# Two gate tiles of the differential heads moved to the end of the delta stage, and ScalarE's and VectorE's order changed there

## The chip, the cores and the metric

The kernel runs on one core of one Trainium2 chip. The metric is the device time of one execution in microseconds. Before the change it is 2049.99 us, the median of 3 runs (2049.94 to 2050.85).

## What is computed

Two transformer blocks follow one another on 512 tokens of width 1024, all in float32. The change lies in the first block. Cut to what matters there:

```python
proj = h @ w_in                        # q, k, v, z, beta, alpha of 4 delta heads; q, k, v, z of 4 differential heads
# group 1, gated delta rule, 4 heads of 128, chunk by chunk, with a state carried on:
#   solve (I + strict(k_beta k^T * decay)) [u, w] = [v_beta, k_beta e^g]
#   v_new = u - w S;  o = (q e^g) S + (q k^T * decay) v_new;  S = S e^g_last + k_dec^T v_new
o_dn = rmsnorm(o) * silu(z_dn)
# group 2, differential attention, 4 heads, query blocks of 128:
#   p = softmax(q1 k1^T) - lam * softmax(q2 k2^T)   (causal);  o = p v
o_df = rmsnorm(o) * (1 - lambda_init) * silu(z_df)
x = x + concat(o_dn, o_df) @ w_out
```

The second block (a feed-forward part, retention and sparse attention, a second feed-forward part) follows and is not touched.

## The kernel before

**Matrix products.** Every large product is made of three matmuls in a reduced float format: a high and a low part of the weights and of the activations (`mm3`, line 2015). The weights come as a stream of 304 blocks of 128 x 1024 in the order of use, into a ring of 4 buffers. SP issues their DMAs (line 796), ScalarE makes the high part (`w_split`, line 807), GpSimd the low part in four pieces (line 2529), TensorE uses them. A *unit* is one `mm3` of 128 rows of the contraction with 512 tokens; a tile of 128 output columns takes 8 units, the values of the differential heads (`dv`) 32.

**The delta stage** (some 99 to 372 us). Four chunks of 128 tokens are worked through one after another. For each chunk, TensorE makes the decay transposes and two score products (gcb, N0, A0), then inverts the triangular matrix in five levels: product Z, copied out by ScalarE (line 1064); transposes Tt, copied out by VectorE (line 1560); product dU, subtracted by VectorE (line 1567). Then come u and wT, the two half chunks with the state (wS, dS) and the output o. Each step waits for the engine before it.

**What fills the gaps.** Every engine's program calls its own `aside()` at 18 *points* per chunk, numbered on from -2 (`POINTS`, line 221). In the call of point p, TensorE (line 2105) issues in this order: the dense units due at p; the sums over squares of a head norm; at even points from 36 on also the scores S of differential step s, the transposes PT of the probabilities of step s - 2 and the product PV of step s - 3. In a level, the odd point lies between Z and dU, the even point between dU and the next Z. Which units are due where is computed in `dense_points` (line 236) from `ASIDE_DENSE` (the order of the tiles), `STRETCHES` (how many units from which point to which) and `SHARE` (weight of each of the 18 points). The order of the tiles is dqk 0, dqk 4, dz 0 to 3, dv, dqk 1, 5, 2, 6, 3, 7, z 0 to 3. `dqk` are the queries (0 to 3) and keys (4 to 7) of the differential heads, `dz` their gates, `z` the gates of the delta heads.

**ScalarE in point p** (`aside`, line 989): first `chains(p)`, line 1010: squares for norms, rsqrt of norms (Ln and Exp), at points 23, 25, 27 and 29 the silu of one `dz` tile each; at odd points from 36 on the two exponentials of step s, which wait for VectorE's maxima, and then the copy of the transposed probabilities PT of step s - 2 into `prob_t` (line 1050). After `chains`: the copy of a tile of dense results out of its PSUM bank when its last unit is due at p (line 1007), then the weight splits that have come due.

**VectorE in point p** (line 1464): scalings by finished norms; at odd points from 36 on the probabilities of step s - 1 (lines 1483 to 1490), then the maxima of step s (line 1500), then the copy of PV (line 1510).

**PSUM banks** are given out by `PLACE` (line 388). The small products of the delta stage, the sums of the head norms among them, take banks 5, 6 and 7 in turn. S uses banks 0 and 1, PT bank 2, PV bank 3, the dense tiles mostly bank 4. `begin(key)` waits until what was in the bank has been copied out.

**Norms of heads.** `norm_point(i)` gives the point of the squares of dqk tile i; the sum is one point later, the rsqrt two, the scaling three. `HO_POINT` (line 270) gives the same start for the norms of outputs: delta chunks 0 to 2 and differential heads 0 to 2 (numbered 4 to 6). The norms of delta chunk 3 and of head 7 come after the last point.

**The output projection** (372 to 423 us) multiplies eight heads' gated outputs, in the order `HEADS_OUT` (line 273): 4, 5, 6, then 0, 1, 2, 3, 7. VectorE gates a head (line 1624), ScalarE makes its high part (line 862) and VectorE its low part (line 1299). TensorE runs columns 0 to 3 over the first three heads, then columns 0 to 3 over the other five, then columns 4 to 7 over all (lines 2241 to 2245). ScalarE makes the silus of the four `z` tiles there (line 1086), one for each head, each followed by the high part of the head before.

Of the kernel before, what the change touches and what calls it, by code (L numbers as in the profile page):

```python
# [37 lines left out]
P = 128  # L38
D = 1024
KD = D // P  # L40
T = 512
# [169 lines left out]
def norms_after(j):  # L211
# [10 lines left out]
ASIDE_DENSE = [("dqk", 0), ("dqk", 4)] + [("dz", j) for j in range(4)] + [("dv", 1)] + \  # L222
    [("dqk", j + c) for j in range(1, 4) for c in (0, 4)] + [("z", j) for j in range(4)]
# [3 lines left out]
STRETCHES = [(8, -2, -2), (6, -1, -1), (82, 0, 38), (16, 39, 46), (16, 47, 54), (32, 55, 70)]  # L227
# [42 lines left out]
HO_POINT = {**{n: POINTS * (n + 1) + 2 for n in range(NQ - 1)}, **{4 + j: DF_START + 8 * j + 14 for j in range(3)}}  # L270
LATE_HEADS = [3, 7]
SILU_POINT = {23 + 2 * j: j for j in range(4)}
HEADS_OUT = [4, 5, 6, 0, 1, 2, 3, 7]
# [117 lines left out]
for _key, _ in RESULTS:  # L391
# [4 lines left out]
    elif _key in ASIDE_DENSE:  # L396
        _p = {("dv", 1): (2, 2), ("dqk", 4): (0, 1), ("dz", 1): (0, 1), ("dz", 3): (0, 1), ("dqk", 5): (2, 1)}.get(_key, (4, 1))
# [147 lines left out]
def build(nc, w_dram, x_dram, meta_dram, const_dram, small_dram, rot_dram, dec_dram, out_dram):  # L545
    with ExitStack() as ctx:
# [256 lines left out]
        def _(act):  # L803
# [206 lines left out]
            def chains(p):  # L1010

                for i in norm_at(p, 0):
                    A.sync()
                    squares([dqk[:, i, :]])
                for i in norm_at(p, 2):
                    rsqrt(("hn", 8 + i), 1.0 / 64, T)
                for i, first in HO_POINT.items():
                    if p == first and i < 4:
                        A.sync()
                        squares_chunk(i)  # L1020
                    elif p == first:
                        wait_evac(act, ("PV", i - 4, NQ - 1))
                        squares([dqk[:, i - 4, :]])
                    elif p == first + 2:
                        rsqrt(("ho", i), 1.0 / P, T)
                if p in SILU_POINT:
                    made["table"] = None
                    j = SILU_POINT[p]
                    A.own(nc.scalar.activation(dsz[:, j, :], dsz[:, j, :], ACT.Silu))
                    if j == 3:  # L1030
                        A.sync()
                        act.sem_inc(s_silu, 1)
# [3 lines left out]
                if s is not None:  # L1036
# [3 lines left out]
                    for c in range(2):  # L1040
                        A.sig(nc.scalar.activation(Sx[i][c][:, 0:w], Sx[i][c][:, 0:w], ACT.Exp, bias=mx[i][:, c:c + 1],  # L1041
                                                   accum_out=sums_[i][:, c:c + 1]), s_dfa, 2 * s + c + 1)
                e = df_at(p, 2)
# [37 lines left out]
            for i in (4, 5, 6):  # L1081
# [206 lines left out]
        def _(dve):  # L1288
# [175 lines left out]
            def aside():  # L1464
# [10 lines left out]
                if p < DF_START or (p - DF_START) % 2 == 0:  # L1475
                    return
                e = df_at(p, 1)
# [13 lines left out]
                s = df_at(p, 0)  # L1491
                if s is not None:
                    j, n, i = s // NQ, s % NQ, s % 2
                    w = (n + 1) * P
                    key = ("S", j, n)
                    if s >= 2:
                        wait_result(dve, ("PT", (s - 2) // NQ, (s - 2) % NQ))
                    wait_result(dve, key)
                    for c in range(2):
                        ins = nc.vector.tensor_tensor_reduce(Sx[i][c][:, 0:w], slot(key)[:, c * 512:c * 512 + w],  # L1500
                                                             K("causal")[:, T - w:T], 1.0, NEG, ALU.add, ALU.max, mx[i][:, c:c + 1])
                        V.own(ins) if c == 0 else V.sig(ins, *evac_at(key))
                    V.sync()
                    V.sig(nc.vector.tensor_scalar(mx[i][:], mx[i][:], -1.0, None, ALU.mult), s_df, 2 + s)
# [105 lines left out]
            def head_out(i):  # L1610
                def maker(dst, m):
# [7 lines left out]
                    if i < 4:  # L1619
                        dve.wait_ge(s_silu, 8 + 2 + i)  # L1620
# [5 lines left out]
            for part in (HEADS_OUT[0:3], HEADS_OUT[3:KD]):  # L1626
# [377 lines left out]
        def _(pe):  # L2004
# [657 lines left out]
```

## Time and profile before

| | us |
|---|---|
| median of 3 runs | 2049.99 |
| profiled execution | 2050.15 |
| its span, first to last instruction | 2048.4 |
| TensorE busy | 1994.2 (97%) |
| GpSimd busy | 936.8 (46%) |
| VectorE busy | 863.3 (42%) |
| ScalarE busy | 735.9 (36%) |

The mean granted TensorE clock is 0.995 of full speed. In the profile's rows PE is TensorE's matmuls, PEld its weight loads, DVE VectorE, ACT ScalarE, POOL GpSimd. The first line number is that of the kernel; many matmuls have line 2013, that of a helper, and are told apart by their tiles. The delta stage's tiles have names of their own buffers: `dn_y` is the copy of Z, `dn_inv_t` U, `dn_inv` Tt, `dn_qg` the exponential of gcb, `score` and `mx` the differential scores and maxima, `slot` is any PSUM bank. A row of the timeline has start, duration, engine, line and operation, and in brackets how long the engine was idle before it and what ended that. The starts of matmuls tell more than their durations, since one begins while the one before still drains.

### The profile page before, as it was taken

To read this page: it belongs to the slowest core of one execution; us is meant where nothing else is said; L and a number is where in the kernel's file an instruction comes from. 1 tells how busy PE (TensorE), PEld (TensorE's weight loads), DVE (VectorE), ACT (ScalarE), POOL (GpSimd) and SP (SyncE) were. 2 spreads that over 40 slices of the span, in tenths; PEclk is the share of its full clock that TensorE was granted. 3 is DMA by queue.
4 is the path that set the end of the run, shared out by engine and by line. 5 is a ranking of instruction groups with operands and counts; after the bars stand their busy time and mean duration, and the time that the engine had idled before them with its cause. 6 is when DMAs were issued, how large, how long until landed. Compare 5 with 4: busy or idle time off the path is not lost.

```text
span 2048.4 us, 30374 instructions
## 1 busy us (share of the span) xinstructions
PE 1994.2 (97%) x11366; PEld 1704.6 (83%) x11366; DVE 863.3 (42%) x1502; ACT 735.9 (36%) x1116; POOL 936.8 (46%) x1220
## 2 busy tenths in 40 slices
PE   7999988999999999999999999999999999999998
PEld 6688666799999999688888888888888888888887
DVE  7744665742222222996443233343343452222112
ACT  5543444432222223634444233333333332222222
POOL 5432211454444564554332545444444564545564
PEclk9999999999999999999999999999999999999999
DMA  5211100122222223222111322222222223222232
GB/s 186 83 62 42 42 32 32 50 95 85 93 88 92 97 99 114 73 83 79 58 61 52 109 72 88 83 78 83 84 77 77 91 90 102 92 92 93 103 103 83
DMA packets 49754, 168.68 MB, mean 82 GB/s; under 512 B 6400, under 2 KB 8576, under 8 KB 49664
## 3 DMA queue, kind: packets, MB, share of 16 engines
q1 hardware_dynamic: 46192, 161.37, 23.4%
q10 hardware_dynamic: 3472, 6.03, 0.9%
q8 instruction: 66, 1.08, 0.2%
q14 instruction: 24, 0.20, 0.0%
HBM read 165.29 MB, written 2.10 MB: 82 GB/s over the span
## 4 chain that ended last, share of the span: by engine, by line
PE 87%; DVE 8%; ACT 2%; issue 1%; DMA 1%; ACTq 0%; DVEq 0%
PE slot L2013 86%; DVE ix_score L1835 1%; DVE square L1770 1%; DVE score L1500 0%; DVE x_lo L1788 0%; DVE xt L1780 0%; ACT score L1041 0%; PE slot L2150 0%; DMA h<-x_t 0%; PE slot L2185 0%; PE slot L2448 0%; DVE dqk L1343 0%; DMA w_raw<-weights 0%; DVE aq L1773 0%; DVE ak L1773 0%
## 5 line engine op out<-in xcount | busy, mean ns | idle before, releaser
L2529 POOL TENSOR_TENSOR w_lo<-w_raw,w_hi 128x256 fp32r<-128x256 f32 x1216 | 936.6, 802 | 1100.9 <-ACT w_hi L814 848.4
L2013 PE MATMUL slot<-x_hi,w_hi 128*128 128x264 f32 (+1 forms) x1864 | 643.9, 345 | 3.5 <-ACT dqk L1007 3.4
L2013 PE MATMUL slot<-x_hi,w_lo 128*128 128x264 f32 (+1 forms) x1864 | 630.5, 338 | 0.0
L2013 PE MATMUL slot<-x_lo,w_hi 128*128 128x264 f32 (+1 forms) x1864 | 628.8, 337 | 0.0
L2013 PEld LDWEIGHTS slot<-x_hi,w_hi 128*128 128x128 f32 x1864 | 351.4, 189 | 50.7 <-issue 7.9
L2013 PEld LDWEIGHTS slot<-x_lo,w_hi 128*128 128x128 f32 x1864 | 350.9, 188 | 39.2
L2013 PEld LDWEIGHTS slot<-x_hi,w_lo 128*128 128x128 f32 x1864 | 351.7, 189 | 37.8 <-issue 1.4
L814 ACT ACTIVATE w_hi<-w_raw 128x1024 fp32r<-128x1024 f32 x216 | 226.4, 1054 | 321.4 <-PE slot L2013 311.6
L2013 PE MATMUL slot<-f_hi,w_hi 128*128 128x264 f32 (+2 forms) x550 | 173.5, 316 | 0.0
L2013 PE MATMUL slot<-f_hi,w_lo 128*128 128x264 f32 (+2 forms) x550 | 173.3, 315 | 0.0
L2013 PE MATMUL slot<-f_lo,w_hi 128*128 128x264 f32 (+2 forms) x550 | 172.9, 314 | 0.0
L1682 DVE TENSOR_TENSOR xt<-slot,rs 128x528 f32<-128x528 f32 (+1 forms) x44 | 30.8, 700 | 218.2 <-PE slot L2013 218.2
L2013 PEld LDWEIGHTS slot<-f_lo,w_hi 128*128 128x128 f32 x550 | 103.5, 188 | 7.1
L2013 PEld LDWEIGHTS slot<-f_hi,w_hi 128*128 128x128 f32 x550 | 103.5, 188 | 7.0
L2013 PEld LDWEIGHTS slot<-f_hi,w_lo 128*128 128x128 f32 x550 | 103.3, 188 | 6.5
L2013 PE MATMUL slot<-w_hi,x_hi 128*128 128x512 f32 (+1 forms) x288 | 103.1, 358 | 4.2 <-DVE ak L1773 4.2
L895 ACT ACTIVATE f_hi<-xt 128x528 f32 (+3 forms) x44 | 28.1, 639 | 217.0 <-DVE xt L1685 217.0
L2013 PE MATMUL slot<-w_hi,x_lo 128*128 128x512 f32 (+1 forms) x288 | 98.9, 343 | 0.0
L2013 PE MATMUL slot<-w_lo,x_hi 128*128 128x512 f32 (+1 forms) x288 | 98.8, 343 | 0.0
L1708 DVE SCALAR_TENSOR_TENSOR h<-slot,h 128x528 f32<-128x528 f32 (+2 forms) x17 | 11.4, 668 | 192.7 <-PE slot L2013 192.7
L883 ACT ACTIVATE w_hi<-w_raw 128x1024 fp32r<-128x1024 f32 x88 | 91.9, 1044 | 0.0
L2013 PE MATMUL slot<-mixed_hi,w_hi 128*128 128x512 f32 x168 | 69.8, 415 | 11.4 <-POOL w_lo L2529 9.4
(342 smaller groups left out, 2819.3 us busy)
## 6 DMA issues: line engine op xcount, KB each, us to landing
w_raw<-weights SPq DMA_DIRECT2D x304, 512.0 KB, 3.2
h<-x_t ACTq DMA_DIRECT2D x4, 512.0 KB, 6.1
dec<-decays ACTq DMA_DIRECT2D x4, 264.0 KB, 3.2
const<-consts SPq DMA_DIRECT2D x1, 576.0 KB, 6.4
at_rot<-rotations ACTq DMA_DIRECT2D x1, 528.0 KB, 5.1
ix_rot<-rotations ACTq DMA_DIRECT2D x1, 528.0 KB, 6.6
rt_rot<-rotations ACTq DMA_DIRECT2D x1, 528.0 KB, 3.7
out<-h SPq DMA_DIRECT2D x2, 256.0 KB, 2.2
```

Source lines behind the costliest of these rows:

```text
L814: nc.scalar.activation(w_hi[b % RING][:], w_raw[b % RING][:], ACT.Copy).then_inc(s_hi, 1)
L883: nc.scalar.activation(w_hi[b % RING][:], w_raw[b % RING][:], ACT.Copy).then_inc(s_hi, 1)
L895: nc.scalar.activation(f_hi[:, g * 2 + (first + j), c0:TT], xt[j][:, c0:TT], ACT.Copy).then_inc(s_xhi, 1)
L1682: nc.vector.tensor_tensor(oo, psu, nn, ALU.mult).then_inc(evac_in(up, g)[0], 1)
L1708: V.sig(nc.vector.scalar_tensor_tensor(hh, src, 0.5, hh, ALU.mult, ALU.add), *evac_at(key))
L1770: V.own(nc.vector.tensor_tensor(other[rows], other[rows], tab(1)[rows], ALU.mult))
L1835: ins = nc.vector.scalar_tensor_tensor(score[n - 1][:, 0:w], relu[s % 2][:, a, 0:w], iw[:, n, 2 * j + a:2 * j + a + 1], before, ALU.mult, ...
L2013: return nc.tensor.matmul(out, lhsT, rhs, start=start, stop=stop)
L2529: nc.gpsimd.tensor_tensor(w_lo[j][:, piece], w_raw[j][:, piece], w_hi[j][:, piece].bitcast(F32), ALU.subtract).then_inc(s_lo, 1)
```

## The change

The tiles dz 2 and dz 3 leave their place ahead of `dv` and come after dqk 7; the stretches are set anew. Their silus move from the delta stage to the output projection, whose first part takes two heads instead of three. ScalarE's `chains` is split up: in a point, the copy into `prob_t` now comes first, then the rsqrts, the dense copies and weight splits, then the squares (those of the next point) and the silus, and the exponentials last. VectorE makes the maxima of step s before the probabilities of step s - 1. The norms of the heads' outputs 4 to 6 start one point later.

```diff
-ASIDE_DENSE = [("dqk", 0), ("dqk", 4)] + [("dz", j) for j in range(4)] + [("dv", 1)] + \
-    [("dqk", j + c) for j in range(1, 4) for c in (0, 4)] + [("z", j) for j in range(4)]
+ASIDE_DENSE = [("dqk", 0), ("dqk", 4)] + [("dz", 0), ("dz", 1), ("dv", 1)] + \
+    [("dqk", j + c) for j in range(1, 4) for c in (0, 4)] + [("dz", 2), ("dz", 3)] + [("z", j) for j in range(4)]
-STRETCHES = [(8, -2, -2), (6, -1, -1), (82, 0, 38), (16, 39, 46), (16, 47, 54), (32, 55, 70)]
+STRETCHES = [(8, -2, -2), (6, -1, -1), (66, 0, 38), (16, 39, 44), (16, 45, 50), (48, 51, 70)]
-HO_POINT = {**{n: POINTS * (n + 1) + 2 for n in range(NQ - 1)}, **{4 + j: DF_START + 8 * j + 14 for j in range(3)}}
+HO_POINT = {**{n: POINTS * (n + 1) + 2 for n in range(NQ - 1)}, **{4 + j: DF_START + 8 * j + 15 for j in range(3)}}
-SILU_POINT = {23 + 2 * j: j for j in range(4)}
-HEADS_OUT = [4, 5, 6, 0, 1, 2, 3, 7]
+SILU_POINT = 23
+LATE_SILUS = [0, 1, 6, 2, 3, 7]
+HEADS_OUT = [4, 5] + LATE_SILUS
+OUT_FIRST = 2
...
-        _p = {("dv", 1): (2, 2), ("dqk", 4): (0, 1), ("dz", 1): (0, 1), ("dz", 3): (0, 1), ("dqk", 5): (2, 1)}.get(_key, (4, 1))
+        _p = {("dv", 1): (2, 2), ("dqk", 4): (0, 1), ("dz", 1): (0, 1), ("dqk", 5): (2, 1)}.get(_key, (4, 1))
...
-                chains(p)
+                prob_copy(p)
+                rsqrts(p)
                 for key in ASIDE_DENSE:
                     if dense_done(key) == p:
...
                 w_split(BLOCK[ASIDE_DENSE[0]] + aside_blocks(p + 1) + RING - 1)
+                all_squares(p)
+                exps(p)
...
+            def all_squares(p):
+
+                for i in norm_at(p, -1):
+                    A.sync()
+                    squares([dqk[:, i, :]])
+                for i, first in HO_POINT.items():
+                    if p == first - 1 and i < 4:
                         A.sync()
                         squares_chunk(i)
-                    elif p == first:
+                    elif p == first - 1:
                         wait_evac(act, ("PV", i - 4, NQ - 1))
                         squares([dqk[:, i - 4, :]])
+                if p == SILU_POINT:
                     made["table"] = None
+                    for j in range(2):
+                        A.own(nc.scalar.activation(dsz[:, j, :], dsz[:, j, :], ACT.Silu))
+                    A.sync()
+                    act.sem_inc(s_silu, 1)
...
-            for i in (4, 5, 6):
+            for i in HEADS_OUT[0:OUT_FIRST]:
                 x_high(1, i, M, mixed_hi)
             rsqrt(("ho", 7), 1.0 / P, T)
             made["table"] = None
-            for j in range(4):
-                A.own(nc.scalar.activation(sz[:, :, j, :], sz[:, :, j, :], ACT.Silu))
+            for i, hd in enumerate(LATE_SILUS):
+                z = sz[:, :, hd, :] if hd < 4 else dsz[:, hd - 4, :]
+                A.own(nc.scalar.activation(z, z, ACT.Silu))
                 A.sync()
                 act.sem_inc(s_silu, 1)
-                if j:
-                    x_high(1, j - 1, M, mixed_hi)
-            for i in (3, 7):
-                x_high(1, i, M, mixed_hi)
+                if i:
+                    x_high(1, LATE_SILUS[i - 1], M, mixed_hi)
+            x_high(1, LATE_SILUS[-1], M, mixed_hi)
...
             for j in range(4):
-                out_part(j, 0, 3)
+                out_part(j, 0, OUT_FIRST)
             for j in range(4):
-                out_part(j, 3, KD)
+                out_part(j, OUT_FIRST, KD)
```

On VectorE the block of the probabilities (`e = df_at(p, 1)`, lines 1477 to 1490) moves behind the block of the maxima (`s = df_at(p, 0)`, lines 1491 to 1504), unchanged; and `head_out` waits for the silu of every head in `LATE_SILUS`.

## Rows read from the trace of the kernel before

**Rows 1.** Windows: length, busy (count) of PE, PEld, DVE, ACT, POOL, PEclk, DMA, GB/s

```profile
109.90:161.70 51.80, 50.77 (x303) 42.24 (x302) 26.42 (x40) 17.44 (x26) 18.11 (x23) 1.00 0.19 63
161.70:213.80 52.10, 51.13 (x325) 44.28 (x324) 24.26 (x39) 18.43 (x26) 12.21 (x16) 1.00 0.14 50
213.80:291.30 77.50, 68.26 (x392) 51.63 (x391) 46.37 (x116) 37.18 (x78) 15.23 (x20) 0.98 0.10 35
291.30:372.00 80.70, 71.89 (x413) 56.08 (x411) 48.62 (x127) 34.99 (x77) 15.99 (x20) 0.94 0.09 29
...
396.00:423.00 27.00, 27.00 (x125) 22.40 (x124) 26.58 (x30) 8.21 (x10) 22.26 (x23) 1.00 0.37 124
```

**Rows 2.** TensorE's waits, 214 to 291 us: total, times, longest

```profile
PE slot L2150 <- ACT prob_t L1050: 3.7, 4, 1.6
PE slot L2013 <- ACT dqk L1007: 3.4, 1, 3.4
PE slot L2013 <- ACT square L834: 1.2, 1, 1.2
PE slot L2013 <- ACT dn_y L1064: 0.7, 1, 0.7
```

**Rows 3.** TensorE's waits from 291 to 372 us

```profile
PE slot L2150 <- ACT prob_t L1050: 4.7, 4, 2.1
PE slot L2013 <- ACT dn_qg L1059: 2.3, 1, 2.3
```

**Rows 4.** Timeline around one such wait, VectorE, ScalarE and TensorE

```profile
253.62 0.75 DVE L1489 SCALAR_TENSOR_TENSOR score<-score,sum 128x512 f32<-128x512 f32 x1
...
254.83 0.17 DVE L1504 TENSOR_SCALAR mx<-mx 128x2 f32<-128x2 f32 x1
...
255.81 0.47 ACT L1050 ACTIVATE prob_t<-slot 128x384 f32<-128x384 f32 x1
...
256.43 0.63 PE L2150 MATMUL slot<-const,score 128*128 128x128 f32 x4 [0.71 <-ACT prob_t L1050]
```

**Rows 5.** Windows with a lowered granted clock (the number after POOL's count)

```profile
280.00:285.00 5.00, 4.75 (x16) 3.40 (x16) 0.00 (x0) 2.35 (x4) 2.80 (x4) 0.67 0.00 0
296.00:302.00 6.00, 4.63 (x18) 3.19 (x19) 5.72 (x9) 4.47 (x8) 3.17 (x4) 0.73 0.01 3
...
357.00:364.00 7.00, 7.00 (x26) 5.91 (x26) 3.17 (x7) 0.33 (x1) 0.00 (x0) 0.53 0.00 0
...
377.00:381.00 4.00, 4.00 (x12) 3.03 (x11) 2.15 (x4) 3.70 (x6) 0.00 (x0) 0.57 0.02 4
```

**Rows 6.** Timeline of TensorE: a half step with one unit, and a sum over squares

```profile
132.44 0.39 PE L2013 MATMUL slot<-x_hi,w_lo 128*128 128x512 f32 x1
132.67 0.40 PE L2013 MATMUL slot<-x_lo,w_hi 128*128 128x512 f32 x1
133.19 1.13 PE L2013 MATMUL slot<-dn_y,dn_inv 128*128 128x128 f32 x8
...
317.43 1.02 PE L2013 MATMUL slot<-square,const 128*128 128x512 f32 x2
318.28 1.05 PE L2013 MATMUL slot<-dn_y,dn_inv 128*128 128x128 f32 x8
```

**Rows 7.** Timeline of TensorE, the first Z of chunk 1

```profile
170.10 1.13 PE L2013 MATMUL slot<-dn_inv_t,dn_join 128*128 128x128 f32 x8 [0.72 <-DVE dn_qg L1552]
```

**Rows 8.** Timeline of VectorE, the copy of U0 in chunk 3

```profile
304.54 0.69 DVE L1555 COPY dn_inv_t<-slot 128x512 f32<-128x512 f32 x1 [0.34 <-PE slot L2177]
```

**Rows 9.** Timeline of the output projection, VectorE and TensorE

```profile
382.66 0.68 DVE L1299 TENSOR_TENSOR mixed_lo<-xt,mixed_hi 128x512 fp32r<-128x512 f32 x1
...
383.98 0.69 DVE L1299 TENSOR_TENSOR mixed_lo<-xt,mixed_hi 128x512 fp32r<-128x512 f32 x1
...
385.87 0.39 PE L2013 MATMUL slot<-mixed_hi,w_hi 128*128 128x512 f32 x1
...
386.10 1.47 DVE L1299 TENSOR_TENSOR mixed_lo<-xt,mixed_hi 128x512 fp32r<-128x512 f32 x2
```

More of the change, by code:

```diff
@@ L1008, in aside, with rsqrts @@
                 w_split(BLOCK[ASIDE_DENSE[0]] + aside_blocks(p + 1) + RING - 1)
[L1010 to L1014, printed above, removed]
+                all_squares(p)
+                exps(p)
+            def rsqrts(p):
                 for i in norm_at(p, 2):
@@ L1017, in chains, with exps @@
                 for i, first in HO_POINT.items():
-                    if p == first and i < 4:
+                    if p == first + 2:
+                        rsqrt(("ho", i), 1.0 / P, T)
+            def all_squares(p):
[4 more added lines that the diff above has]
+                    if p == first - 1 and i < 4:
                         A.sync()
                         squares_chunk(i)
-                    elif p == first:
+                    elif p == first - 1:
                         wait_evac(act, ("PV", i - 4, NQ - 1))
                         squares([dqk[:, i - 4, :]])
-                    elif p == first + 2:
-                        rsqrt(("ho", i), 1.0 / P, T)
-                if p in SILU_POINT:
+                if p == SILU_POINT:
                     made["table"] = None
[L1028 to L1032, printed above, removed]
+                    for j in range(2):
+                        A.own(nc.scalar.activation(dsz[:, j, :], dsz[:, j, :], ACT.Silu))
+                    A.sync()
+                    act.sem_inc(s_silu, 1)
+            def exps(p):
                 if p < DF_START or (p - DF_START) % 2 == 0:
@@ L1042, in chains, with prob_copy @@
                                                    accum_out=sums_[i][:, c:c + 1]), s_dfa, 2 * s + c + 1)
+            def prob_copy(p):
+                if p < DF_START or (p - DF_START) % 2 == 0:
+                    return
                 e = df_at(p, 2)
@@ L1476, in aside @@
                     return
-                e = df_at(p, 1)
-                if e is not None:
-                    j, n, i = e // NQ, e % NQ, e % 2
-                    w = (n + 1) * P
-                    dve.wait_ge(s_dfa, 2 * e + 2)
-                    V.own(nc.vector.reciprocal(sums_[i][:], sums_[i][:]))
-                    V.sync()
-                    V.own(nc.vector.tensor_scalar(sums_[i][:, 1:2], sums_[i][:, 1:2], lamt[:, 5:6], None, ALU.mult))
-                    V.sync()
-                    V.own(nc.vector.tensor_scalar(Sx[i][1][:, 0:w], Sx[i][1][:, 0:w], sums_[i][:, 1:2], None, ALU.mult))
-                    V.sync()
-                    V.sig(nc.vector.scalar_tensor_tensor(Pm[i][:, 0:w], Sx[i][0][:, 0:w], sums_[i][:, 0:1], Sx[i][1][:, 0:w],
-                                                         ALU.mult, ALU.add), s_dfp, e + 1)
                 s = df_at(p, 0)
@@ L1504, in aside @@
                     V.sig(nc.vector.tensor_scalar(mx[i][:], mx[i][:], -1.0, None, ALU.mult), s_df, 2 + s)
+                e = df_at(p, 1)
+                if e is not None:
+                    j, n, i = e // NQ, e % NQ, e % 2
+                    w = (n + 1) * P
+                    dve.wait_ge(s_dfa, 2 * e + 2)
+                    V.own(nc.vector.reciprocal(sums_[i][:], sums_[i][:]))
+                    V.sync()
+                    V.own(nc.vector.tensor_scalar(sums_[i][:, 1:2], sums_[i][:, 1:2], lamt[:, 5:6], None, ALU.mult))
+                    V.sync()
+                    V.own(nc.vector.tensor_scalar(Sx[i][1][:, 0:w], Sx[i][1][:, 0:w], sums_[i][:, 1:2], None, ALU.mult))
+                    V.sync()
+                    V.sig(nc.vector.scalar_tensor_tensor(Pm[i][:, 0:w], Sx[i][0][:, 0:w], sums_[i][:, 0:1], Sx[i][1][:, 0:w],
+                                                         ALU.mult, ALU.add), s_dfp, e + 1)
                 e = df_at(p, 3)
@@ L1618, in maker @@
                         V.sync()
-                    if i < 4:
-                        dve.wait_ge(s_silu, 8 + 2 + i)
+                    if i in LATE_SILUS:
+                        dve.wait_ge(s_silu, 8 + 2 + LATE_SILUS.index(i))
                     z = sz[:, :, i, :] if i < 4 else dsz[:, i - 4, :]
@@ L1625, in head_out @@
                 return maker
-            for part in (HEADS_OUT[0:3], HEADS_OUT[3:KD]):
+            for part in (HEADS_OUT[0:OUT_FIRST], HEADS_OUT[OUT_FIRST:KD]):
                 split([head_out(i) for i in part], M, 0, mixed_hi, mixed_lo, part)
```

## The prediction, made before the result was known

> **What bounds the kernel now.** I read first the busy time by stage, then the list of TensorE's waits in the last two chunks of the delta stage, then the order of time around some of those waits. The windows [rows 1] cut the delta stage at the transposes that open its four chunks: 51.8, 52.1, 77.5 and 80.7 us. In chunks 0 and 1 TensorE lacks 1.0 us each of being busy throughout, in chunk 2 it lacks 9.2, in chunk 3 8.8. From 396 us on it is busy without a gap, and the change touches nothing there: what can be won is idle time and slow clock before that point.
>
> The waits of chunk 2 [rows 2] and chunk 3 [rows 3] name the causes. Eight waits of the differential transposes on the copy of the previous transposed probabilities (prob_t) cost 3.7 + 4.7 us; one wait for a tile copied out of its PSUM bank (dqk) 3.4; squares of a chunk 1.2; the copy of the delta's Z (dn_y) 0.7; the exponential that frees the bank of gcb (dn_qg) 2.3. One such wait in order of time [rows 4]: VectorE ends the probabilities at 254.37 and the maxima at 255.00, only then ScalarE takes the two exponentials and, behind them, the copy (255.81), and TensorE starts its transposes at 256.43. The copy's own input had been there since the even point before: it stands behind the exponentials only by its place in ScalarE's program.
>
> Idle time is not all. The granted clock [rows 5] was 0.67 for 5 us after the 3.4 us wait, 0.73 for 6 us around the 2.3 us wait, 0.53 for 7 us late in chunk 3 and 0.57 for 4 us in the output projection, which is 1.6, 1.6, 3.3 and 1.7 us of lost work (length times one minus the clock); these are stretches at 1.2 GHz among others at 2.4.
>
> **Prices.** A dense unit is three matmuls of 512 columns, which start 0.23 us apart (132.44 to 132.67): 0.69 us [rows 6]. A sum over squares takes TensorE 0.85 us (317.43 to 318.28) [rows 6]; I take 0.9 with its start. I counted units and sums by laying the table of points out. The dense units go from 38, 36, 38, 34 in chunks 0 to 3 to 31, 30, 45, 40: 13 units, 8.9 us, leave the first two and enter the last two. (The two tiles are 16 units; the end of the dv tile and of dqk shift with the new stretches.) The sums go from 6 to 8 in chunk 2 and from 5 to 3 in chunk 3.
>
> **Chunk 0: -4.1 us.** 7 units leave: -4.8. In a half step with one unit TensorE waits for the copies: its last dense matmul starts at 132.67 and would hand over 0.23 later, the next one starts at 133.19, so 0.3 us are lost [rows 6]. There are two more such half steps: +0.6. A unit before the first Z saves only half, since that Z waits for VectorE: +0.35. One unit more ahead of the chunk's output covers a wait of about 0.3 there.
>
> **Chunk 1: -1.4 us.** 6 units leave: -4.1. Two of them stood before the first Z, which already waited 0.72 for VectorE [rows 7], so they save nothing: +1.4. Three half steps fall to one unit: +0.9. One before the last output also: +0.4. From both sides: chunks 0 and 1 together give between 0 (VectorE and ScalarE bound them as soon as cover goes) and -8.9 (units alone); I take -5.5, nearer the units, since the gap that [rows 6] show with one unit is less than half of a unit.
>
> **Chunk 2: -2.5 us.** The probability copy now comes first in its point, a point before it is needed: -3.7. The dense copies come before the exponentials: the dqk wait, -3.4, and its slow clock, -1.6. Squares move to the end of the point before: -1.2. Z's copy no longer has a chain of table load and squares before it: -0.7. Against that 7 units +4.8 and 2 sums +1.8. New waits: a sum now stands right behind the transposes of gcb at the chunk's start and needs their bank, the situation that cost 2.3 in chunk 3. Here two dense units stand before it in both cases, but no differential probabilities delay VectorE yet, so it is nearer to half: I take 1.0, and 0.5 for the maximum that S of the next point waits for. Bounds 0 and 2.8.
>
> **Chunk 3: -6.0 us.** Waits -4.7 and -2.3 (no sum stands there any more); slow clock -1.6 and -3.3; 2 sums -1.8; 6 units +4.1. At the chunk's start VectorE is the bound: its copy of U0 at 304.54, which the first Z needs, follows an idle time of only 0.34 [rows 8], and its work there does not shrink; two head scalings now even fall between gcb and T. TensorE, with one wait and two sums fewer, arrives early and waits: +2.4, between 0 and 3. A wait of that size was followed by a slow stretch three times [rows 5]; I book 1.2, as part of it lies beside VectorE's work; bounds 0 and 3.3.
>
> In both chunks VectorE takes the maxima before the probabilities, which makes the latter later by the maxima: 0.63 us in [rows 4], where the block is the narrowest, and by my estimate from that up to 1.4 where it is four times as wide. There it is covered: probabilities were ready 2.06 us before the transposes that used them. The maxima, and so the exponentials, come earlier, and the exponentials, though now behind a dense copy and a weight split, are needed two points later. Booked at nothing, covered by the 2 or 3 dense units and the S of the even point; with no cover it would be the third rival.
>
> **Output projection: +2.0 us.** The first part now has 2 heads (8 units, 5.5 us) instead of 3, the second six. VectorE makes a head each 1.32 us (382.66 to 383.98) [rows 9], TensorE uses one in 0.69 us for a column. So the first column waits. ScalarE drops one copy before the last rsqrt, so the first late head comes sooner, but it is one head more, and the last low part stays where it was, at 387.57 [rows 9]. The first column then ends a unit after that part is ready, at 388.3, instead of 389.3 (385.87 [rows 9] plus 5 units), and the three others have a unit more each, 2.1: +1.1. The short waits may add a slow stretch to the one shown: 0 to 1.7, I take 0.9. The silus removed at points 27 and 29 hid under matmuls there, so they give nothing; at the end two more silus on ScalarE hide beside VectorE's 1.32 per head.
>
> **Queues.** The weight blocks keep their number; two of them move behind dqk 7 in the stream, with their DMA on SP, the split on ScalarE and four subtractions on GpSimd. No row of [rows 2, 3] is a wait for the low part, so I book nothing; if it were late, TensorE's first unit of a tile would show it. One tile moves from bank 0 to bank 4; it must wait for the copy of the tile before, which has a Z, dU or output matmul in between: nothing.
>
> **Sum.** -4.1 - 1.4 - 2.5 - 6.0 + 2.0 = -12.0 us. The profiled execution took 2050.15 (span 2048.4 and 1.75 around it), 0.16 above the median of 2049.99. 2050.15 - 12.0 = 2038.15, or 2038.0 against the median; I forecast **2038.0**.
>
> **Rivals.** A difference under 0.2% (4.1 us) can't be told from none here.
> 1. The first two chunks give nothing, as their chain bounds them once the cover is thin: +5.5, 2043.5. For it: chunk 1 starts with a wait for VectorE already [rows 7]. Against: the gap of [rows 6] is 0.3. Chance 0.14.
> 2. VectorE becomes the bound of chunks 2 and 3, so that half of the eight waits (4.2) come back under its name, with a slow stretch or two (3.3): 2045.5, on the border. For it: 48.6 us busy of 80.7 [rows 1], in one chain with TensorE. Chance 0.12.
> 3. Slower: the probabilities, now behind the maxima, are what each of the 16 transposes waits for. Price up to 16 x 1.1 = 17.6: 2055.5. It decides from 0.8 us a transpose on. Against: the 2.06 us of [rows 4]. Chance 0.04.
> 4. The short waits in the thinned chunks 0 and 1 bring the clock down. Each fall costs 1.6 to 3.3 us, so three would give about 2045, eight would cancel all. Against: the granted clock was 1.00 over both chunks [rows 1] although half steps with such gaps were there. The Trainium skill (TensorE: Matmul & The Clock Gate, A second HAM failure mode) says that frequent micro-idles between groups of matmuls can make the clock swing though the engine looks busy; by that rule the thinning is harmful, and no run here shows it at gaps of 0.3 us. Chance 0.06.
> 5. All waits go and none of the new ones comes (no slow stretch at chunk 3's start or in the projection, no wait for VectorE): -12.0 - 1.2 - 0.9 - 2.4 - 1.5 = -18.0, 2032.0. Chance 0.14.
> The copies could also fail to come earlier, if their input came only in their own point; the order of the program (transposes in the even point, copy in the odd one) excludes it.
>
> My forecast (2035 to 2042) has 0.5. The range 2031.5 to 2046.0 takes in rivals 1 and 5 and the better parts of 2 and 4. Faster 0.85 (the forecast, 1, 5 and the better half of 2), the same 0.10 (the rest of 2, most of 4), slower 0.05 (3, and the worst of 4).
>
> **What would show it.** Right: no wait of the transposes on prob_t but in the last point, no wait on dqk; chunk 0 near 47.7, chunk 1 near 50.7, chunk 2 near 75, chunk 3 near 74.5 us; a wait for VectorE ahead of chunk 3's first Z; waits on mixed_lo in the first column. Wrong: waits of transposes on the probabilities (VectorE), a clock below 1.00 in chunks 0 or 1, or a projection later than 2 us.

## The result, and the profile after

The changed kernel takes **2039.09 us** (median of 5 runs), the kernel before 2049.94 beside it: ratio 0.9946, 95% interval 0.9935 to 0.9957. The forecast was 2038.0 with a range of 2031.5 to 2046.0. The profiled execution took 2037.25 (span 2035.5), 12.9 less than the 2050.15 of before; the steps below are measured against these two. It is the shortest of its five executions (2037.25 to 2040.2), so the steps sum to 2.0 more than the 10.85 us by which the medians differ. Of the 12.9, 0.5 come from ahead of the delta stage, which the change doesn't touch; over all the profiles below that point, the start of chunk 0, lies between 109.19 and 110.59 us.

First a correction of my own reading. The cut at 213.80 in [rows 1] lies 1.5 us late: chunk 2's transposes of gcb start at 212.26. Chunk 3 had been cut at 372.00 instead of at its last product with the values (370.50). The forecasts of the chunks' lengths are to be read from these cuts: the changes in length of the prediction give 47.7, 49.2, 76.6 and 73.2 us. The windows of before with all cuts made alike:

```profile
161.70:212.26 50.56, 49.59 (x312) 42.74 (x310) 23.39 (x37) 17.09 (x24) 12.21 (x16) 1.00 0.15 52
212.26:291.33 79.07, 69.83 (x405) 53.17 (x404) 47.27 (x118) 38.52 (x79) 15.23 (x20) 0.98 0.10 34
291.33:370.50 79.17, 70.36 (x403) 54.89 (x402) 48.30 (x126) 34.38 (x77) 15.99 (x20) 0.94 0.08 27
370.50:396.00 25.50, 23.45 (x93) 17.64 (x94) 19.29 (x28) 15.57 (x23) 5.29 (x6) 0.93 0.07 21
```

And the windows of after, which answer to them and to [rows 1] (length, busy time of PE, PEld, DVE, ACT, POOL, then the granted clock):

```profile
109.36:156.99 47.63, 46.32 (x282) 38.14 (x281) 25.32 (x40) 15.62 (x23) 14.62 (x19) 1.00 0.20 65
156.99:206.68 49.69, 46.57 (x293) 38.99 (x292) 24.98 (x37) 18.33 (x25) 13.01 (x16) 1.00 0.12 37
206.68:283.81 77.13, 74.70 (x430) 57.18 (x429) 48.53 (x123) 39.18 (x83) 15.65 (x20) 1.00 0.11 40
283.81:357.05 73.24, 69.58 (x418) 55.69 (x416) 47.69 (x120) 32.86 (x73) 18.74 (x24) 0.98 0.11 37
357.05:382.00 24.95, 21.33 (x86) 15.10 (x87) 19.67 (x29) 16.60 (x25) 5.89 (x6) 1.00 0.08 25
```

The third window is to be read as a pair with its row of before: TensorE is busy 4.87 us longer, and idle 2.43 us instead of 9.24. The moved work and the filled gaps nearly cancel. What is left of the waits in the stage and the projection, against [rows 2, 3]:

```profile
PE slot L2029 <- DVE mixed_lo L1315: 3.3, 4, 1.5
PE slot L2029 <- DVE dn_qg L1568: 2.3, 1, 2.3
PE slot L2029 <- DVE mx L1502: 1.9, 1, 1.9
PE slot L2029 <- ACT rs L853: 1.6, 1, 1.6
PE slot L2029 <- ACT prob_t L1066: 1.2, 1, 1.2
...
PE slot L2166 <- DVE score L1519: 0.3, 1, 0.3
```

The eight waits of the transposes (8.4 us under a helper's line of their own, now 2166) are gone, and so are dqk, dn_y and the long dn_qg of ScalarE; the prob_t left is that of the last product with the values. In order of time, one round as in [rows 4], then the waits that are left:

```profile
252.16 0.59 ACT L1066 ACTIVATE prob_t<-slot 128x512 f32<-128x512 f32 x1
...
253.52 0.17 DVE L1506 TENSOR_SCALAR mx<-mx 128x2 f32<-128x2 f32 x1
254.36 0.35 DVE L1519 SCALAR_TENSOR_TENSOR score<-score,sum 128x128 f32<-128x128 f32 x1
...
255.85 0.50 ACT L1052 ACTIVATE score<-score,mx 128x256 f32<-128x256 f32 x1
...
279.61 0.60 ACT L1088 ACTIVATE qkv<-slot 128x512 f32<-128x512 f32 x1 [5.54 <-PE slot L2029]
280.10 0.48 ACT L1066 ACTIVATE prob_t<-slot 128x384 f32<-128x384 f32 x1
280.47 0.69 ACT L853 ACTIVATE rs<-slot,eps 128x512 f32<-128x512 f32 x1
281.22 1.16 PE L2029 MATMUL slot<-xt,dn_kdec 64*128 64x128 f32 x8 [1.64 <-ACT rs L853]
...
296.22 0.92 PE L2029 MATMUL slot<-dqk 64*128 64x384 f32 x4 [1.92 <-DVE mx L1502]
297.44 0.33 PE L2166 MATMUL slot<-const,score 128*128 128x128 f32 x1 [0.31 <-DVE score L1519]
...
361.90 0.47 PE L2029 MATMUL slot<-mixed_hi,w_hi 128*128 128x512 f32 x1 [1.46 <-DVE mixed_lo L1315]
```

The copy of the probabilities (252.16) now comes 1.36 us ahead of the maxima. The row at 281.22 is the one wait that I hadn't seen coming: the second half chunk's product for the state (dS) needs a bank that holds sums of squares, and the rsqrt that frees it stands in ScalarE's program behind the copy of the chunk's output (279.61), which is itself late work of that chunk.

### The profile page after: what moved, and what is told of

It reads as the page before. It is cut to its first block, busy times and chain, and to the rows that moved or that the text cites. A ratio compares the mean times of both kernels' runs of the same rounds, so it can differ in the third digit from the quotient of the medians.

```text
span 2035.5 us, 30377 instructions
## 1 busy us (share of the span) xinstructions
PE 1991.9 (98%) x11366; PEld 1702.1 (84%) x11366; DVE 863.6 (42%) x1502; ACT 735.5 (36%) x1116; POOL 939.7 (46%) x1220
## 4 chain that ended last, share of the span: by engine, by line
PE 91%; DVE 5%; ACT 2%; issue 1%; DMA 1%; ACTq 0%; DVEq 0%
PE slot L2029 90%; DVE x_lo L1804 0%; DVE square L1786 0%; DVE xt L1796 0%; DMA h<-x_t 0%; PE slot L2464 0%; PE slot L2201 0%; DVE dqk L1359 0%; PE slot L2166 0%; ACT rs L853 0%; DMA w_raw<-weights 0%; DVE qkv L1409 0%; DVE ak L1789 0%; DVE ix_score L1851 0%; DVE xt L1640 0%
```

## The experiments

The kernel's time is split at the same points in each profile: the start of each chunk's gcb transposes, the last product with the values (chunk 3's end), the first matmul of the projection, and the logarithm of FFN 1's norm ("projection" is the time between these last two). From there to the end every kernel takes 1619.3 to 1620.0; between chunk 3's end and the projection lie 4.9 us in all but order_best2 (6.3). Each row is one execution, and executions of one kernel differ: those of order_both_back run from 2043.28 to 2049.48. A difference of 2 us between two rows is therefore read together with the medians.

| kernel | chunk 0 | 1 | 2 | 3 | projection | span | median, ratio [95%] |
|---|---|---|---|---|---|---|---|
| before | 51.80 | 50.56 | 79.07 | 79.17 | 53.16 | 2048.4 | |
| after | 47.63 | 49.69 | 77.13 | 73.24 | 54.09 | 2035.5 | 2039.09, 0.9946 [0.9935, 0.9957] |
| order_alone | 51.78 | 50.55 | 72.52 | 70.87 | 52.33 | 2032.1 | 2032.52, 0.9911 [0.9894, 0.9927] |
| tiles_alone | 47.69 | 51.21 | 86.63 | 81.57 | 54.10 | 2056.2 | 2058.01, 1.0044 [1.0029, 1.0058] |
| projection_alone | 51.81 | 50.55 | 80.68 | 79.15 | 56.22 | 2052.5 | 2053.29, 1.0015 [1.0006, 1.0025] |
| copy_last | 47.61 | 49.72 | 78.44 | 72.03 | 54.10 | 2035.9 | 2038.51, 0.9944 [0.9927, 0.9961] |
| maxima_second | 47.69 | 49.72 | 77.36 | 74.04 | 54.10 | 2037.1 | 2039.26, 0.9947 [0.993, 0.9963] |
| norm_point_undone | 47.65 | 49.73 | 75.44 | 71.31 | 54.10 | 2031.9 | 2034.86, 0.9929 [0.9912, 0.9945] |
| old_tiles_copy_behind | 51.81 | 50.55 | 72.30 | 70.40 | 52.30 | 2031.6 | 2035.09, 0.9934 [0.9917, 0.9951] |
| old_tiles_exps_early | 51.79 | 50.55 | 73.60 | 70.88 | 52.33 | 2033.8 | 2036.17, 0.9934 [0.9917, 0.9951] |
| order_both_back | 51.80 | 50.53 | 76.45 | 78.13 | 52.33 | 2044.0 | 2046.66, 0.9986 [0.9976, 0.9996] |
| order_sum_table | 51.75 | 50.54 | 69.55 | 68.34 | 52.30 | 2027.6 | 2029.48, 0.9901 [0.9885, 0.9918] |
| order_best2 | 51.78 | 50.54 | 69.50 | 68.11 | 52.79 | 2028.3 | 2030.18, 0.9906 [0.989, 0.9923] |

**The two halves of the change.** First the new order alone, on the tiles, stretches and projection of before (with it VectorE's maxima ahead of the probabilities):

```diff
-                chains(p)
+                prob_copy(p)
+                rsqrts(p)
...
+                all_squares(p)
+                exps(p)
```

> The kernel before with the changed order of ScalarE and VectorE alone (tiles, stretches, silus and the projection's order as before). Theory 1, the order and the moved tiles both earn: the waits of the transposes on prob_t and the one on dqk go (8.4 and 3.4 us, with 1.6 and 3.3 of slow clock), but with 13 units less in the last two chunks TensorE comes to VectorE's and ScalarE's results early and waits about 0.5 us a level (10 levels), so the time is 2041 to 2044, later than the full change. Theory 2, the order earns all and the tiles' move only shifts work: 2033 to 2037, earlier than the full change, as the first chunks lose 5 us but the last two carry 8.9 us of units and the projection 0.9 less. Chunks 0 and 1 are 51.8 and 50.6 us in both.

Then the tiles, stretches, silus and projection of after under the old order of ScalarE and VectorE (on after, the same edit the other way round):

```diff
-                prob_copy(p)
-                rsqrts(p)
+                chains(p)
...
-                all_squares(p)
-                exps(p)
```

> The full change with the old order on ScalarE and VectorE (copy into prob_t behind the exponentials and ahead of the dense copies, squares at a point's start, probabilities before maxima). Theory 1: chunks 0 and 1 stay at 47.6 and 49.7 us; in chunks 2 and 3 the waits on prob_t shrink with the cover from 8.4 to some 3 us, the wait for a dense copy (3.4) stays or comes at several tiles; 2045 to 2049. Theory 2: no gain at all or a loss, 2049 to 2054. Either way waits of the transposes on prob_t are back in the list.

The order alone gives 16.3 us by the profiles and 18.2 by the medians (2032.52 beside 2050.7); the tiles alone (the shifted norms are in it) cost 7.8 and are slower outside the interval. On the new tiles the order is worth 20.7 (2056.2 to 2035.5). Both lie outside what was expected: the order a little under the 2033 to 2037 of its second theory, the tiles (2058.01) above even the 2049 to 2054 of theirs. TensorE's waits between 205 and 400 us, first of the order alone, then of the tiles alone:

```profile
PE slot L2031 <- ACT dn_qg L1076: 2.2, 1, 2.2
PE slot L2031 <- DVE mixed_lo L1317: 2.0, 3, 1.5
PE slot L2031 <- ACT dn_y L1081: 2.0, 1, 2.0
PE slot L2031 <- ACT prob_t L1067: 1.2, 1, 1.2
```

```profile
PE slot L2029 <- ACT dqk L1012: 6.2, 2, 3.7
PE slot L2166 <- ACT prob_t L1066: 4.8, 5, 1.6
PE slot L2029 <- ACT qkv L1012: 3.7, 1, 3.7
...
PE slot L2029 <- DVE mx L1516: 2.2, 2, 1.7
...
PE slot L2029 <- ACT dsz L1012: 1.2, 1, 1.2
```

With the old order the added units of chunks 2 and 3 buy little: prob_t waits fall from 8.4 to 4.8 us, but copies of dense tiles, of which there are more there now, are awaited four times (dqk twice, qkv and dsz, a dz tile, once each) for 11.1 us in place of 3.4. The longest, in ScalarE's order: the dense copy stands behind exponentials that themselves waited for the maxima.

```profile
233.38 0.61 ACT L1052 ACTIVATE score<-score,mx 128x384 f32<-128x384 f32 x1 [2.98 <-DVE mx L1520]
...
234.59 0.25 ACT L1066 ACTIVATE prob_t<-slot 128x128 f32<-128x128 f32 x1
234.75 0.58 ACT L1012 ACTIVATE dqk<-slot 128x512 f32<-128x512 f32 x1
...
235.38 0.79 PE L2029 MATMUL slot<-x_hi,w_hi 128*128 128x512 f32 x1 [3.69 <-ACT dqk L1012]
```

Chunk 1 of tiles_alone took 51.21 us where 49.7 was expected. Its waits are those of after, the same one of 2.3 us ahead of the first Z; but here a lowered clock followed it, where after has 1.00 from 165 to 170:

```profile
166.71 2.05 PE L2029 MATMUL slot<-dn_inv_t,dn_join 128*128 128x128 f32 x8 [2.31 <-DVE dn_qg L1568]
```

```profile
165.00:170.00 5.00, 3.29 (x12) 3.03 (x13) 2.21 (x3) 0.60 (x1) 2.80 (x3) 0.66 0.22 60
```

**The projection alone**: on before, only the later silus and the new split of the heads.

```diff
-SILU_POINT = {23 + 2 * j: j for j in range(4)}
-HEADS_OUT = [4, 5, 6, 0, 1, 2, 3, 7]
+SILU_POINT = {23: 0, 25: 1}
+LATE_SILUS = [0, 1, 6, 2, 3, 7]
+HEADS_OUT = [4, 5] + LATE_SILUS
+OUT_FIRST = 2
```

> The kernel before with the projection's change alone: first part over two heads, the silus of dz 2 and dz 3 at the end. The delta stage keeps its lengths (51.8, 50.6, 79.1, 79.2). From the first matmul of the projection to the rsqrt of the first feed-forward part it was 53.2 us before (with 1.7 of slow clock) and is 54.1 in the full change (no slow clock). By my sum the projection costs 1.1 without the clock and up to 2.0 with it: 2051 to 2053. If the clock is what decides, the interval is 54.1 again and the time 2050.5 to 2052; if the projection cost nothing, 53.2 or less and 2049 to 2051.

The stretch takes 3.06 us more than before, and 2.12 more than the same code in after; mixed_lo waits are 3.3 us in both. Of these 2.12, 1.7 are the clock: 0.73 in this window of projection_alone and 0.93 in the next five microseconds, while after has 1.00 over the whole stretch. The time, 2053.29, is just above the 2051 to 2053 expected; its ten executions run from 2049.36 to 2055.18.

```profile
386.00:391.00 5.00, 3.86 (x12) 2.64 (x11) 3.60 (x7) 1.44 (x2) 0.00 (x0) 0.73 0.00 0
```

(The 80.68 of its chunk 2 against 79.07, with the same waits, lie outside the edit.)

**Which element of the order?** Each was taken back by itself in the changed kernel: the probability copy behind the exponentials,

```diff
-                prob_copy(p)
                 rsqrts(p)
...
                 exps(p)
+                prob_copy(p)
```

> The full change with one thing undone: the copy into prob_t stands last in ScalarE's point again, behind dense copies, squares and exponentials. If the place of this copy was the cause of the eight waits, they come back, 4 to 10 us in chunks 2 and 3 together with slow clock, 2043 to 2050. If the better cover and the earlier maxima hide them anyway, it is within 2 us of the full change, 2037 to 2041.

and VectorE's probabilities ahead of the maxima (the two blocks swapped back):

```diff
+                e = df_at(p, 1)
...
                 s = df_at(p, 0)
...
-                e = df_at(p, 1)
```

> The full change with one thing undone: VectorE makes the probabilities before the maxima again. My sum booked this order at nothing. If so, 2037 to 2041, with the wait on the maxima at chunk 3's start (1.9 us) a little longer, 3 us, as they come later. If the maxima first is what hides the exponentials, waits on mx or on exponentials come at many points and it is 2042 or more. If it had cost something (probabilities late), the 0.3 us wait on score goes and it is 0.3 to 1 us faster.

Neither makes a difference that can be told from after: 2038.51 and 2039.26. In copy_last the copy's waits come back at 1.7 us (three of them), and the wait for the maxima at chunk 3's start falls by as much, from 1.9 to 0.2; in maxima_second chunk 3 starts on the maxima 3.0 us late instead of 1.9. The same was then asked on the old tiles, where there is less cover in chunks 2 and 3; first the copy behind (the edit of copy_last, on order_alone),

> order_alone with the copy into prob_t last in ScalarE's point, so without the cover of the moved tiles. In the full change this place cost nothing over the whole (1.7 us of waits on prob_t against 1.7 less on the maxima). If the copy's place matters once TensorE has 34 to 38 units instead of 40 to 45, waits of the transposes on prob_t of 4 to 8 us are back and it takes 2036 to 2041. If it was never the place of the copy but the wait for the dense copies and the maxima, it stays within 2 us of order_alone, 2031 to 2035.

then the exponentials ahead of the dense copies:

```diff
                 rsqrts(p)
+                exps(p)
...
                 all_squares(p)
-                exps(p)
```

> order_alone with the exponentials ahead of the dense copies, weight splits and squares (the copy into prob_t stays first). If the dense copies' place behind the exponentials is the dear part of the old order (waits of 3.4 us on a dense tile, with slow clock), chunk 2 gets one or two of them back, 4 to 8 us: 2037 to 2041. If the copy into prob_t was the dear part, it stays at 2031 to 2035.

The copy behind brings back 2.5 us of prob_t waits in four places, yet its profile (2031.6) is no longer than that of the order alone (2032.1). The clock hides it: around the waits on dn_y and dn_qg, which both kernels have, order_alone ran at 0.86 and 0.80 (226 to 236) and at 0.66 (290 to 295), old_tiles_copy_behind at 1.00 each time. The medians (2035.09, 2032.52) are 2.6 apart, with overlapping intervals. So this place of the copy costs about 2.5 us, which lies between the two expectations. The exponentials ahead bring back half of the dqk wait (1.7 us, before 3.4): 1.7 us by the profiles, 3.6 by the medians (its executions, 2034.99 to 2037.43, all lie above those of order_alone, 2031.26 to 2033.90). So no single element that was taken back carries the 16 us. The theory that was left: the probabilities, the maxima, the exponentials and the copy stood in one chain over two engines, and cutting it in one place does most of it. It was tested with both taken back at once, on order_alone (the edits of copy_last and maxima_second together):

> The order change alone, but with two of its elements taken back at once: VectorE takes the probabilities ahead of the maxima again, and ScalarE copies the transposed probabilities behind the exponentials again. The squares stay at the end of the point before, and the copies of dense tiles stay ahead of the exponentials. Theory 'one chain, cut at two places': VectorE's probabilities, its maxima, ScalarE's exponentials and the copy stood in one chain before the differential transposes; each of the two elements alone had cut it, so the wait comes back only when both are taken back. Then waits of the transposes on prob_t of 5 to 8.4 us in chunks 2 and 3 (8.4 before), at least four of them, and a time of 2039 to 2044 us, that is 4 to 8 us above the order change alone (2032.5). Rival 'neither matters; the squares and the dense copies ahead of the exponentials earn it all': prob_t waits stay at 2.5 us or less, as with the copy alone taken back, and the time is 2032 to 2036 us. A wait on the copied bank (dqk) is expected by neither.

```profile
PE slot L2168 <- ACT prob_t L1067: 10.0, 10, 2.2
PE slot L2031 <- ACT dn_qg L1076: 2.2, 1, 2.2
PE slot L2031 <- ACT dn_y L1081: 2.0, 1, 2.0
```

The waits are back in full, ten of them, and the time is 2046.66, 2.7 us above what the chain theory had said and far outside its rival. There are ten waits and not eight; here the copy stands behind the dense copies too, as it didn't in before, which may be why. Taken back one at a time the elements cost 2.6 us (the copy, on the old tiles) and nothing that can be told (the copy and the maxima, on the new tiles); together they are worth 14 us by the medians (2046.66 to 2032.52) and 12 by the profiles. The maxima alone on the old tiles were not run, so it is not excluded that there the maxima's place alone carries most of it. The rest of the gain, 3.2 us (2046.66 to 2049.88), is of the size that the exponentials ahead of the dense copies cost alone; the moved squares were not taken back by themselves.

**The wait that I had not seen coming**, in after: the norms of heads 4 to 6 back to their old point, so that their sums don't share point 52 with another sum.

```diff
-{4 + j: DF_START + 8 * j + 15 for j in range(3)}
+{4 + j: DF_START + 8 * j + 14 for j in range(3)}
```

> The full change with the norms of heads 4 to 6 one point earlier again, so that point 52 has one sum and not two. If the unforeseen wait of 1.6 us on an rsqrt at the end of chunk 2 comes from two sums there and the bank that one of them holds until ScalarE's rsqrt behind the output copy, it goes, chunk 2 is 75.3 to 76 us long and the time 1 to 2 us below the full change, 2036 to 2038. If it comes from the bank rotation as such, the wait moves to another product and chunk 2 stays at 77.

The wait of 1.64 us is gone and chunk 2 is 1.69 shorter. Chunk 3 is 1.93 shorter, though it waits for the maxima as long as in after. The median, 2034.86, is below the 2036 to 2038 expected, and its executions (2033.72 to 2036.2) all lie below those of after. The window behind that wait in after, and the same stretch with the wait in norm_point_undone:

```profile
296.00:301.00 5.00, 4.47 (x20) 3.73 (x21) 4.75 (x18) 2.52 (x6) 2.00 (x3) 0.68 0.01 2
```

```profile
292.00:297.00 5.00, 2.78 (x18) 1.75 (x17) 4.75 (x16) 2.52 (x6) 0.01 (x1) 1.00 0.01 2
297.00:302.00 5.00, 5.00 (x31) 4.15 (x30) 4.27 (x12) 2.40 (x6) 2.84 (x4) 1.00 0.17 54
...
294.20 0.92 PE L2029 MATMUL slot<-dqk 64*128 64x384 f32 x4 [1.91 <-DVE mx L1502]
```

**A version that beats both.** The waits that order_alone has left point to it: a sum directly behind the chunk's transposes (dn_qg, 2.2) and a load of ScalarE's function table (1.28 us) in the chain ahead of Z's copy (dn_y, 2.0).

```diff
-    return p + 1 if (p + 1) % POINTS == POINTS - 1 else p
+    return p + 2 if (p + 1) % POINTS == POINTS - 1 else p
...
+                if made["table"] != LN_EXP:
+                    nc.scalar.preload_act_table_set(LN_EXP)
+                    made["table"] = LN_EXP
                 act.wait_ge(s_dn, dnv("dt", n))
```

> The order change alone with two small edits: the sum of differential head 3's norm stands a point later (point 55 in place of 54, so behind the first Z of chunk 3 and not directly behind its gcb transposes, with its copies and rsqrt a point later), and the table of exp and ln is loaded ahead of the chunk's own exponentials in the first chunk point of a round, not ahead of the norm's logarithm. Theory: the wait of 2.2 us at the start of chunk 3 (290.82, released by the exponential of gcb) goes with the slow stretch behind it, and the Z copy's wait (dn_y 2.0 in chunk 2) falls to about 0.7: chunk 3 is 68 to 69.5 us instead of 70.87, chunk 2 71.3 to 72 instead of 72.52, the time 2028.5 to 2031 us. Rival: VectorE, which delivers U0 for chunk 3's first Z, is the bound there anyway (booked in the prediction), so the wait only changes its name and the time stays at 2032 to 2033.5 us.

Its chunks 2 and 3, and the waits of the two that are left:

```profile
212.88:282.43 69.55, 68.42 (x406) 52.47 (x405) 48.05 (x118) 37.11 (x79) 14.71 (x20) 1.00 0.12 39
282.43:350.77 68.34, 65.66 (x403) 51.30 (x402) 48.28 (x126) 34.16 (x76) 15.89 (x20) 1.00 0.10 32
...
PE slot L2034 <- ACT dqk L1010: 0.8, 1, 0.8
...
PE slot L2034 <- ACT dn_y L1084: 0.6, 1, 0.6
```

2029.48 us, ratio 0.9901 [0.9885, 0.9918]: its interval lies below that of the change as made. It overlaps that of order_alone, but the executions don't: 2028.3 to 2029.63 against 2031.26 to 2033.90. The theory gave chunk 3 rightly (68 to 69.5). Chunk 2 became 2.97 us shorter where 0.5 to 1.2 were expected: 1.4 are the shorter wait on dn_y, the rest is the clock, which order_alone had at 0.98 over this chunk (0.86 and 0.80 in the ten microseconds from 226, around that wait at 228.39) and this kernel at 1.00. (The clock's part belongs to these two executions: old_tiles_copy_behind has the same wait on dn_y with the clock at 1.00.) The rival, VectorE as the bound at chunk 3's start, falls for this order of work: from 282.43 to 300 TensorE waits once, 0.8 us for dqk. One step more, two units to the last two points as cover for the last wait on prob_t:

```diff
-..., (16, 47, 54), (32, 55, 70)]
+..., (16, 47, 54), (32, 55, 72)]
```

> The run before this one (sum a point later, table ahead of the chunk's exponentials) and two dense units moved out of points 55 to 70 into points 71 and 72, the last of the stage, where PV of the last differential step waited 1.2 us for the copy of its probabilities. Theory: the stage's last steps have a cover of 1.4 us, that wait falls to 0.3 or less and the time is 0.5 to 1.2 us below the run before it, 2027.5 to 2030.5. Rival: the two units are missed where they were, in the rounds of chunk 3, whose short waits then grow by as much: no difference (within 0.5 us) or a wait on the last silus' input at the projection.

```profile
PE slot L2034 <- DVE mixed_lo L1320: 2.0, 1, 2.0
PE slot L2034 <- ACT square L836: 1.4, 1, 1.4
PE slot L2171 <- DVE score L1524: 1.3, 2, 1.1
...
349.66 0.60 ACT L1010 ACTIVATE qkv<-slot 128x512 f32<-128x512 f32 x1 [1.77 <-PE slot L2034]
350.16 1.05 ACT L816 ACTIVATE w_hi<-w_raw 128x1024 fp32r<-128x1024 f32 x1
...
351.10 0.62 ACT L836 ACTIVATE square<-qkv 128x512 f32<-128x512 f32 x1
...
351.87 1.96 PE L2034 MATMUL slot<-square,const 128*128 128x512 f32 x4 [1.35 <-ACT square L836]
```

No gain (2030.18). The wait of 1.2 on prob_t has gone. In its place the sum for delta chunk 3's output waits 1.4 for its squares (351.10), and this is once more a wait of order: their input, the chunk's output, was copied out at 346.81, but with the two units the last dense tile ends later, and its copy and a weight split (349.66, 350.16) now stand ahead of the squares in ScalarE's program. In order_sum_table the same squares ran at 350.75, directly behind the copy into prob_t. The rival has its part too: in chunk 3, where the two units are missed, two waits on the probabilities (1.3) are new. Squares ahead of that last copy and split were not tried.

## Why the prediction was right

| step | forecast | measured |
|---|---|---|
| chunk 0 | -4.1 | -4.17 |
| chunk 1 | -1.4 | -0.87 |
| chunk 2 | -2.5 | -1.94 |
| chunk 3 | -6.0 | -5.93 |
| projection | +2.0 | +0.93 |
| outside the steps | 0 | -0.9 |
| sum | -12.0 | -12.9 |

(From the table above; "outside" is -0.54 ahead of chunk 0, -0.37 behind the projection.) The median of five runs stands 1.84 above the profiled execution; that, and not the steps, puts it 1.1 above the forecast. The chunks' forecasts hold in their sum and in most of their terms; that chunk 2 and the projection came out within 1.1 us is in part luck, as told below.

**Chunks 0 and 1.** Prices by unit and by half step held. The first Z of chunk 1, which already waited for VectorE [rows 7], now waits 2.3 us for it, 1.6 more: the two units that "save nothing" cost that, as booked. Rival 1 (they give nothing) and rival 4 (short waits bring the clock down) fell: the granted clock is 1.00 in both windows, and the gaps of 0.3 us in the half steps with one unit (in after a dense matmul starts at 125.71 and the next product at 126.23, where 0.23 would do) did nothing to it. The rule of the Trainium skill that was weighed there (TensorE: Matmul & The Clock Gate, A second HAM failure mode) was not seen at gaps of this size. The wait of 2.3 us is another matter: behind the same wait tiles_alone shows 0.66 for 5 us and its chunk 1 is 1.5 us longer, so that here part of rival 4 was avoided by luck.

**Chunk 2.** All four waits went as priced. By the pair of windows, busy time rose by 4.87 where units, sums and the faster clock gave +5.0 (4.8 + 1.8 - 1.6). Of the new waits the wrong ones were priced: the sum behind the transposes of gcb waits 0.2 (booked 1.0), the maximum none (booked 0.5), and the rsqrt of head 4 takes 1.64. That 1.8 us of new waits stand where 1.5 were booked is luck. I had moved the norms of heads 4 to 6 only as two sums more in the count; that they fall in one point with another sum, and that their bank then comes free behind the chunk's output copy, was in the table of points that I had laid out, and unread. The unseen edit was worth 3.6 us by the profiles and 4.2 by the medians (norm_point_undone): 1.7 are this wait; the rest is the slow stretch in chunk 3, whose tie to the edit is not shown.

**Chunk 3.** Waits and clock as forecast. The wait for VectorE was booked at 2.4 us ahead of the first Z; it came ahead of S, as 1.92 + 0.31. The slow stretch behind it, booked at 1.2, measured 1.6 (5 us at 0.68). The estimate that probabilities behind the maxima stay covered held (one wait of 0.3); rivals 2 and 3 fell.

**Projection.** The size is off. The schedule costs 1.8 (54.09 against the 52.33 of order_alone, both at full clock) where I had 1.1: the waits on mixed_lo are four with 3.3 us in all, against three with 2.0 in order_alone. The clock went the other way, and made up for it: I booked a further slow stretch of 0.9, and the one of before went too, 0.8 us (53.16 against 52.33). projection_alone shows the case I had booked, slow stretch and all: 3.06 where I had 2.0.

**What the sum hid.** Nearly all terms were right, and still the prediction left out what matters most for judging the change: its terms were added by stage, never by part of the change. Its own numbers say that moving the tiles gives 5.5 in chunks 0 and 1 and costs 8.9 of units and 2.0 in the projection, a loss; the 16 us come from the order. The runs say so: order_alone beats after by 3.4 us by the profiles and 6.6 by the medians, while norm_point_undone, the tiles' move without the shifted norms, is level with order_alone by the profiles (2031.9, 2032.1) and 2.3 above it by medians whose intervals overlap. So the move of the tiles is worth nothing or costs a little, and the shifted norms cost the rest. The waits that the moved units were to cover were gone by the order alone.

## What to carry to other kernels

Before work is moved under a wait as cover, look whether the wait is one of order: an instruction whose input has long been there, behind others in its engine's program. If so, mend the order and leave the work. That holds for cover added at the end as well: two units more moved a dense copy and a weight split ahead of squares whose input was long ready, and TensorE waited for those (order_best2). When a chain runs over two engines, cutting one link can do most of the work, so taking one link back at a time can show each as worth little; take two back together. And add up a forecast by the parts of the change as well as by the stages of the kernel: it tells which part to leave out.

## What the hardware showed that I had not expected

- Behind a wait the clock falls at one time and not at another. The 1.9 us of S for the maxima were followed by a granted clock of 0.68 in after and of 1.00 in norm_point_undone; the 2.3 us in chunk 1 by 1.00 in after and 0.66 in tiles_alone; the 2.0 us for dn_y by 0.86 and 0.80 in order_alone and 1.00 in old_tiles_copy_behind. Executions of one and the same kernel differ by as much: old_tiles_copy_behind took 2033.38 us at a mean clock of 0.999 and 2038.93 at 0.995. What decides it was not isolated. For a forecast it means a chance on 1.6 to 2 us behind each wait, not a price.
- For reading profiles it means that two single profiles can hide a real cost. A difference of 2.5 us in waits (old_tiles_copy_behind against order_alone) did not show in the spans, since the other kernel's profile had two slow stretches; the medians of four showed it.
